# Forgetting attention moved whole beside the projections, and RWKV's units started every ten rounds

## The reference

```python
z = h @ w_in                         # columns: fox (1544), rwkv (1792), gates (2048)
# forgetting attention ("fox"): 8 heads of 64, causal
q = rmsnorm(q, g_q); k = rmsnorm(k, g_k)
c = cumsum(log_sigmoid(zf_last + b_f))
pr = softmax(where(mask, q @ k.T * scale + c[q] - c[k], NEG_BIG))
y_fox = pr @ v
# RWKV-7: 8 heads of 64
zr = zr + mu_shift * (token_shift(zr) - zr)
decay, a, kk, k, v, r = ...          # small low-rank products, elementwise
st = st * w_t + (st @ a_t) b_t + v_t k_t ;  y_t = st @ r_t   # recurrence over tokens
y_rwkv = (group_norm(y) + bonus) * g
merged = sigmoid(zg0) * (y_fox @ w_o_fox) + sigmoid(zg1) * (y_rwkv @ w_o_rwkv)
```

## Time and profile before

| | |
|---|---|
| three runs | 4293.16, 4296.64, 4302.06 us; median 4296.64 |
| profiled execution | 4300.37 us, span of the core 4299.1 us |
| mean granted TensorE clock | 0.938 of full |
| PE busy | 3922.4 us, 91% |
| DVE, ACT, POOL busy | 2143.1, 1157.1, 330.0 us |
| `gates` with 96 rounds of fox | 2438 to 2692 us |
| RWKV with 132 rounds of fox | 2702 to 3245 us |

### The profile page before, as it was taken

The page is one execution under the profiler, slowest core; times in us unless marked ns, Lnnn a source line. Parts: engine busy times, 40 slices in busy tenths (PEclk is TensorE's granted clock), DMA queues, the critical chain, the costliest instruction groups (busy, mean ns, idle before and its releaser), DMA issues. The chain is left out here.

```text
span 4299.1 us, 75536 instructions
## 1 busy us (share of the span) xinstructions
PE 3922.4 (91%) x33542; PEld 3206.1 (75%) x33542; DVE 2143.1 (50%) x3525; ACT 1157.1 (27%) x1597; POOL 330.0 (8%) x362
## 2 busy tenths in 40 slices
PE   6999959986998999999999999778887999999999
PEld 5788837774876888888798677566666788888877
DVE  4633345554433444445624333465554476666774
ACT  4221234442322312121400222242323321111122
POOL 0001102230000000000000000232311000000000
PEclk8999969997998999999999899888787999999999
DMA  5212120114112111111132312201004311111111
GB/s 179 87 52 69 50 84 6 32 32 150 49 40 98 48 51 40 50 48 49 51 133 96 125 67 84 87 23 56 22 10 149 108 48 41 49 49 49 50 45 64
DMA packets 213721, 281.99 MB, mean 66 GB/s; under 512 B 15612, under 2 KB 171004, under 8 KB 213268
## 3 DMA queue, kind: packets, MB, share of 16 engines
q1 hardware_dynamic: 177536, 191.35, 13.8%
q10 hardware_dynamic: 35860, 85.79, 5.3%
HBM read 217.11 MB, written 60.00 MB: 64 GB/s over the span
## 5 line engine op out<-in xcount | busy, mean ns | idle before, releaser
L436 PE MATMUL ps<-sb_a_h,sb_whi 128*128 128x512 f32 x2912 | 1164.5, 400 | 51.0 <-DVE sb_a_h L665 44.6
L437 PE MATMUL ps<-sb_a_h,sb_wlo 128*128 128x512 f32 x2912 | 1146.1, 394 | 0.0
L438 PE MATMUL ps<-sb_a_h,sb_whi 128*128 128x512 f32 x2912 | 1145.5, 393 | 0.0
L436 PEld LDWEIGHTS ps<-sb_a_h,sb_whi 128*128 128x128 f32 x2912 | 552.8, 190 | 195.1 <-issue 53.3
L438 PEld LDWEIGHTS ps<-sb_a_h,sb_whi 128*128 128x128 f32 x2912 | 553.2, 190 | 118.6
L437 PEld LDWEIGHTS ps<-sb_a_h,sb_wlo 128*128 128x128 f32 x2912 | 553.5, 190 | 116.9 <-issue 4.3
L389 ACT ACTIVATE sb_whi<-sb_wraw 128x2048 fp32r<-128x2048 f32 (+3 forms) x146 | 260.4, 1783 | 839.7 <-PE ps L438 512.8
L397 DVE TENSOR_TENSOR sb_wlo<-sb_wraw,sb_whi 128x2048 fp32r<-128x2048 f32 (+3 forms) x146 | 315.8, 2163 | 241.5 <-ACT sb_whi L389 216.0
L548 DVE TENSOR_TENSOR sb_x<-sb_x,ps 128x512 f32<-128x512 f32 x480 | 313.3, 683 | 227.0 <-PE ps L438 224.5
L436 PE MATMUL ps<-sb_a_g,sb_whi 128*128 128x512 f32 x896 | 349.8, 390 | 10.5 <-DVE sb_x L548 10.5
L437 PE MATMUL ps<-sb_a_g,sb_wlo 128*128 128x512 f32 x896 | 348.8, 389 | 0.0
(11 more groups left out here) (513 smaller groups left out, 5567.2 us busy)
## 6 DMA issues: line engine op xcount, KB each, us to landing
sb_wraw<-w_in SPq DMA_DIRECT2D x33, 1024.0 KB, 5.1
sb_wraw<-w_ff SPq DMA_DIRECT2D x32, 1024.0 KB, 5.3
sb_wraw<-w_up SPq DMA_DIRECT2D x22, 1024.0 KB, 5.0
sb_wraw<-w_down SPq DMA_DIRECT2D x11, 1024.0 KB, 4.8
sb_wraw<-w_xkv SPq DMA_DIRECT2D x8, 1024.0 KB, 5.5
sb_wraw<-w_out SPq DMA_DIRECT2D x8, 1024.0 KB, 5.3
sb_a_f<-y ACTq DMA_DIRECT2D x16, 512.0 KB, 4.6
gates<-sb_a_f ACTq DMA_DIRECT2D x32, 256.0 KB, 2.0
```

The source lines that it names most:

```text
L436: e.matmul(o, wh[:, k, c], xh[:, sl], start=(k == 0), stop=False)
L437: e.matmul(o, wl[:, k, c], xh[:, sl], start=False, stop=False)
L438: m = e.matmul(o, wh[:, k, c], xl[:, sl], start=False, stop=(k == t.nk - 1))
```

## The change

Fox is advanced beside the later `shift` tiles (`later = shift[3:]`, 25 tiles) and all 32 `gates` tiles, four rounds per tile (after k = 1, 3, 5 and 7), and what is left of it is run out before RWKV begins. The staging buffers of the projections go from 8 to 6, the banks of `shift` and `lora` are 0 to 3. In fox, AV has v stationary (64 columns) and the transposed probabilities moving (128 columns), the two heads writing the two halves of the partitions; the result comes out already turned, so the transposes of line 2718 and the division at 2755 go. The division is made in the turn: T is an ordinary product of the probabilities with a diagonal matrix that holds the inverse sums (`DG`), which DVE builds after each exponential. A pair has 55 rounds.

RWKV has no fox beside it. `loop` runs 110 rounds; unit i's `pre` and unit i-1's `inner` start every ten rounds, so for five of ten rounds two `inner` streams run; `scan` starts 25 rounds after its unit's `pre`. M, Y, XA, XT and G1 get a second buffer, the rotated r, O and the bonus a third, the two-bank ring becomes (0, 2), the one-bank ring 4 to 7, and the four empty rounds before `pre` go.

```diff
+            later = shift[3:]
+
+            def four(stream):
+                for _ in range(4):
+                    next(stream, None)
...
                 for t in shift:
-                    pe_fm(e, t, hp)
+                    pe_fm(e, t, hp, None, (0, 1, 2, 3), pe_fox, (1, 3, 5, 7) if t in later else ())
...
                 for t in gates:
-                    pe_fm(e, t, hp, None, (0, 1, 2, 3), pe_fox, (2, 5, 7))
+                    pe_fm(e, t, hp, None, (0, 1, 2, 3), pe_fox, (1, 3, 5, 7))
...
                     if t.first:
                         ve_cut(e, t.j + 2)
+                    if t in later:
+                        four(ve_fox)
                     e.wait_ge(*bk.filled(t.key))
...
                         for b in range(0, n, 128):
-                            m = e.transpose(ps[:, b:b + 128], lg_of(p, qb, g)[:, a + b:a + b + 128], C("ident"))
+                            m = e.matmul(ps[:, b:b + 128], lg_of(p, qb, g)[:, a + b:a + b + 128], DG[g], start=True, stop=True)
...
-                    for j in range(qb + 1):
-                        m = e.matmul(bk["fx_y", p, qb // 4][:, c:c + 64], lg_of(p, qb, g)[:, j * 128:(j + 1) * 128],
-                                     R(VF + j * 128 + g * 64, 64), start=(j == 0), stop=(j == qb))
+                for j in range(qb + 1):
+                    for g in range(2):
+                        m = e.matmul(bk[key][64 * g:64 * g + 64, c:c + 128], R(VF + j * 128 + g * 64, 64),
+                                     lg_of(p, qb, g)[:, j * 128:(j + 1) * 128], start=(j == 0), stop=(j == qb))
...
+                for g in range(2):
+                    e.wait_ge(*fx_exp[g].at(8 * p + qb))
+                    e.reciprocal(sinv[:, g:g + 1], R(SUM + (qb % 4) * 2 + g, 1)).then_inc(*vo.up())
+                    e.wait_ge(*vo.last())
...
+                    e.tensor_scalar(DG[g], C("ident"), sinv[:, g:g + 1], None, ALU.mult).then_inc(*fx_dg[g].up())
...
             a4(*fox)
+            for stream in fox:
+                for _ in stream:
+                    pass
             meet()
...
-            RW_REST = 4
+            RW_REST = 0
...
-                for i in range(10):
-                    streams = [scan(i - 2)] if i >= 2 else []
-                    if 1 <= i <= 8:
-                        streams.append(inner(i - 1))
-                    if i < 8:
-                        streams.append(pre(i))
-                    together(*streams, side=fox)
+                running = []
+                for n in range(110):
+                    i, begins = divmod(n, 10)
+                    if n % 10 == 5 and n >= 25 and i - 2 < 8:
+                        running.append((0, scan(i - 2)))
+                    if begins == 0 and 1 <= i <= 8:
+                        running.append((i, inner(i - 1)))
+                    if begins == 0 and i < 8:
+                        running.append((99, pre(i)))
+                    running.sort(key=lambda x: x[0])
+                    for x in list(running):
+                        if next(x[1], running) is running:
+                            running.remove(x)
```

More of the change, by code:

```diff
@@ L2420, in ve_a4 @@
                         ve_cut(e, t.j + 2)
-                    three(ve_fox)
+                    four(ve_fox)
                     e.wait_ge(*bk.filled(t.key))
@@ L2452, in ac_a4 @@
                                     b[0:rows, :]).then_inc(*o.up())
+                for t in first[-2:]:
+                    e.wait_ge(*stored(t.key))
+                e.wait_ge(*x_spilled.at(0))
                 for t in shift:
@@ L2493, in po_a4 @@
                 e.memset(AF[:, 4 * T:4 * T + 3078], 0.0).then_inc(*sh_pad.up())
-                for t in gates:
-                    three(po_fox)
+                for t in later + gates:
+                    four(po_fox)
             def sp_a4(e):
@@ L2499, in sp_a4 @@
                 e.dma_start(WU[64:128, :], D["w_aaa_up_2"]).then_inc(*lora_in.up())
-                sp_load(e, shift[-1].j + 3)
+                sp_load(e, shift[0].j + 3)
                 e.wait_ge(*x_spilled.at(0))
-                e.wait_ge(*bk.filled(shift[-1].key))
-                for t in first[-8:]:
+                for t in first[-6:]:
                     e.wait_ge(*stored(t.key))
-                for t in gates:
+                for t in later + gates:
                     if t.first:
                         sp_load(e, t.j + 3)
-                    three(sp_fox)
+                    four(sp_fox)
             pe_a4(pe), ve_a4(ve), ac_a4(ac), po_a4(po), sp_a4(sp)
@@ L2643, in ve_block @@
                 yield
+                for g in range(2):
+                    e.wait_ge(*fx_exp[g].at(8 * p + qb))
+                    e.reciprocal(sinv[:, g:g + 1], R(SUM + (qb % 4) * 2 + g, 1)).then_inc(*vo.up())
+                    e.wait_ge(*vo.last())
+                    if p or qb:
+                        last = (p, qb - 1) if qb else (p - 1, 7)
+                        e.wait_ge(*bk.filled(("fx_t", *last, g, chunks(last[1])[-1][0])))
+                    e.tensor_scalar(DG[g], C("ident"), sinv[:, g:g + 1], None, ALU.mult).then_inc(*fx_dg[g].up())
                 for a, n in chunks(qb):
@@ L3423, in b2, with loop @@
-            loop(lambda i: pe_pre(pe, i), lambda i: pe_in(pe, i), lambda i: pe_scan(pe, i), fox[0])
-            loop(lambda i: ve_pre(ve, i), lambda i: ve_in(ve, i), lambda i: ve_scan(ve, i), fox[1])
-            loop(lambda i: ac_pre(ac, i), lambda i: ac_in(ac, i), lambda i: ac_scan(ac, i), fox[2])
-            loop(lambda i: po_pre(po, i), lambda i: po_in(po, i), lambda i: po_scan(po, i), fox[3])
+            def loop(pre, inner, scan):
+                running = []
[11 more added lines that the diff above has]
+                            running.remove(x)
+                assert not running
```

183 lines of the change are left out of this document (83 added, 100 removed).

## The result

The kernel after takes 4349.64 us (median of 4 runs, 4344.79 to 4351.09) against 4298.80 us for the kernel before, run beside it (4293.16 to 4302.06): a ratio of 1.0118, 95% interval 1.0100 to 1.0135. I had forecast 4286, slightly faster. It is slower, outside the forecast's own 4255 to 4320 and just at the upper end of the wide range, 4350. The profiled execution took 4348.74 us against 4300.37, 48 us more, and all of it lies in the two stages that the change touches.

The account below looks back on a forecast made before the run. PE alone was taken to bound the projections, a PE, DVE, PE chain RWKV's `inner`. Projections +190 (streams +102, pauses +88) and RWKV -200 gave -10 on a profiled 4300.4: 4286 us predicted, own range 4255 to 4320, 8 in 10 4215 to 4350.

Parts of the forecast that it names:

- Part 1, streams (+102): Projection stage: fox's PE instructions take 39 us a pair, 156 for four pairs, against 54 in the stage before: +102.
- Part 1, pauses (+88): Projection stage: switches, block waits, heads, casts and half-clock time, less overlap, against 26 us before: +88.
- half-clock time, 8: Projection stage, a term of the pauses: some time at half clock after the long stops, 8 us.
- blocks, heads and casts: Projection stage: block waits 16, pair heads 38, casts 14 beside `gates`, 29 beside `shift`, other `shift` pairs 7, less 15 overlap.
- Part 2, the period (38 us): RWKV: six periods of 38 us with two `inner` streams, bounds 33 and 45, making 228 us instead of 385.4.
- The head: RWKV's first twenty rounds: 29 us for `pre` alone, then 26 us for `pre` and one `inner`.
- the tail: RWKV's end, the last `inner` and two `scan`: 60 us, against 57.6 before.
- B: Projections: casts beside `shift` close DVE and ACT to fox, PE's clock falls, stage grows by 250: +50, 4347; chance 0.17.
- C: RWKV: the period stays at 45 us, DVE's and PE's work in one in-order chain: total +32, 4329; chance 0.12.
- A: RWKV: two units abreast interlock fully, 33 us a period, heads and casts cost half: -80, 4217; chance 0.21.
- D: Fox is not done beside the projections; the rest runs alone before RWKV and the -10 gain is gone; chance 0.02.
- Drain ahead of AV 0.35: Projection stage, a sign: PE idles 0.35 us ahead of AV's 16 instructions as the array's shape changes.

Follow-up runs that it names:

- e2: Kernel after, with T as transposes against the identity; diagonal still built and waited for, division left out of the result: 4324.05 us, ratio 1.0037.
- e4: Kernel after, whole computation, with T as transposes and the division made late, as DVE multiplies the turned output by the inverse sums: 4293.53 us, ratio 0.9978.
- e8: e4 with one DVE instruction of RWKV's preparation, the key times the inverse norm, issued one round later: 4295.16 us, ratio 0.9981.
- e10: e5 with two overwritten 128x128 products put ahead of PE's wait for DVE in each of a unit's five levels: 4266.21 us, ratio 0.9909.
- e12: e5 with `pre` ahead of the two `inner` streams in each RWKV round instead of behind them: 4273.96 us, ratio 0.9930.
- e5: e4 with the weight casts' subtraction on POOL instead of DVE as long as fox runs: 4263.75 us, ratio 0.9909.
- e6: e4 with two of the turned tiles copied out three times by DVE in RWKV, 22 us of added work: 4298.53 us, ratio 0.9994.

## Why the prediction was wrong

**Direction and size.** The sum was right in most of its parts and wrong in one quantity that I had at nearly nothing: PE's clock. From the profiled 4300.4 the forecast was 4290, measured 4348.7: 58 us. By the windows +30 is in the projections (220 against 190), +39 in RWKV (161 against 200), and -10 the stretch that the window of before leaves out. With the projections counted to the meeting of the engines in both, they are +21 and +39.

**Part 1, streams (+102): borne out.** At full clock T's four blocks take 0.9 us from start to start (two rows of the timeline of PE, one head each):

```profile
2891.71 1.05 PE L2603 MATMUL ps<-sb_b,sb_x 128*128 128x128 f32 x8
2892.60 1.06 PE L2603 MATMUL ps<-sb_b 128*128 128x128 f32 x8
```

AV is 0.055 us an instruction at full clock where I took 0.045 with the tails, 0.067 over the stage. Fox's streams, from start to start without waits, sum to 166 us (T 76, S 43, AV 39, sums of squares 9) against 54 in the stage before, to the meeting: +112. The excess is the clock: at 0.225 us a block T would be 65. e2 takes 36 us off T's stream, where I had T cost 8.2 x 4 = 33 more, and the stage gives back 21 of them: PE idles 5 us more in e2, and the projections' own matmuls take 10 us longer.

**Part 1, pauses (+88): the waits right, the term "half-clock time, 8" wrong.** PE's idle time sums to 79 us against 17, +62. I had 16 + 38 + 14 + 29 + 7 - 15 = 89 for blocks, heads and casts; the casts' share, read from the ten stops that end at a cast, is 42, against 14 + 29. The projections' own 1368 matmuls take 357 us, 48 more than at 0.226 each, where I had 17 for switches and 8 for the clock; before, to the meeting, they took 321. At full clock they start 0.244 us apart on average against 0.231 before, which is 18 of those 35 us. At the lower level they start some 0.45 apart, and that is the other 17. It isn't all that the clock cost, since fox's own instructions lie at the lower level too. Of PE's busy time 93 us lie there, before 25. Half of such time is lost, 34 us more than before, where the forecast had 8. So the clock was 26 us over, more than the whole miss of 21; without it my sum for this stage was 5 us too high. That is the failed step: I counted each stop once, as idle time, and next to nothing for the slow stretch behind it.

**Part 2, the period (38 us): wrong, by the clock and the idle both.** I wrote that PE's work would be "about 31 at the clock of 0.91", a clock read from the one stretch before without `pre` or fox, and added 7. Measured are 33.8 of work at 0.83, and 9.3 idle. Of the 33.8, 13 stand at the lower level, so at full clock it would be 27.3: the work was right, the clock was not. In the profiled executions of e4 to e8, e10 and e12 the idle time of a period stays between 7.7 and 9.5 us, whatever was added or moved; extra PE work counts 75%, extra DVE work about a third, fewer rounds nothing. What holds that idle time there isn't shown. The head was 8 us over (63 against 55), the tail about right (61 against 60); the five periods and what lies of a sixth ahead of the tail carry 30 of the 39 us.

**Rivals.** B (casts close DVE and ACT to fox, 4347) has the number, by luck: it adds a stage 250 us longer (measured 211 to 220) to an RWKV 200 shorter (161). Its mechanism is there, 42 us of stops and 30 us for taking the subtraction away (e5), but the stops were in my sum already at 43, they last 1.7 to 5.8 us and not 6 to 8, and its point of decision, pauses over 140 us, was not reached (79 idle). What B said in passing, that the clock falls, is what was missing. C (period 45, +32) is nearest for RWKV, 43, and not for its reason: with DVE's and PE's work in one chain e6 would have cost its full 22 us, not 7 (15 at most). A is out: no stretch came near 33. D is out.

**What would show it.** PE busy never under 85% in the projections: held for the whole, 87%, but not for its parts, 82% over each of the first two 100 us. Waits over 100 us: 79, missed. Largest on the diagonal and the sums of squares: held. Drain ahead of AV 0.35: the 0.35 us are there, but they are not PE's (the rows below). Period 38: missed, and just at the bound of 43 that I gave for being wrong. The drain, in the kernel after (start us, us, instruction, idle ahead):

```profile
2861.42 0.40 PE L438 MATMUL ps<-sb_a_h,sb_whi 128*128 128x512 f32 x1
2861.75 0.13 PEld L2616 LDWEIGHTS ps<-sb_x 128*64 128x64 f32 x1 [0.36 <-issue]
2861.75 0.32 PE L2616 MATMUL ps<-sb_x 128*64 128x128 f32 x1
```

The 0.36 us with nothing to wait for stand on the weight loads (PEld). The last projection matmul is still at work then, and PE's own row has no idle time; the 0.36 us of line 2586 in the earlier trace rows stand on a weight load too, and I had read them as PE's. From the start of the last projection matmul to the first of AV it is 0.33 us instead of 0.226, and from the last of AV to the next projection matmul 0.20 instead of 0.055: about 0.25 us a visit. AV comes to 9.7 us a pair all the same, against my 9.3, since its instructions take 0.055 us and not 0.045. The Trainium skill, "TensorEngine Tiling (Array Packing)", "Key Properties", has a change of tiling mode drain the array; the weight loads' wait on nothing agrees. Under "Performance Considerations" it lists this swap with 2x column tiling; AV's instruction went from 0.107 to 0.055 us at full clock, which agrees too, with 8 visits a pair at 0.25 us to set against it.

**What stays open.** In the projections the time at the lower clock goes with PE's idle time. In RWKV the sum of the idle time doesn't tell the clock: over five periods it is 40 us at 0.80 (e8), 43 at 0.81 (e12), 42 at 0.84 (e5), 48 at 0.89 (e6, one execution, with the highest clock of its twelve) and 39 at 0.89 (e10). e10 shows that filling pauses raises the clock. Whether it is where the pauses fall or what PE does when busy that sets it otherwise wasn't told apart.

## What to carry to other kernels

Where PE is the bound and its work is fed by short chains, price each added stop of PE twice: its length, and the work behind it at half clock; in this stage some 34 us came behind 62 us of added stops. Before moving a side stream beside other work, list what stands at the head of each in-order queue that it shares, with the wait that it brings: here a 2.2 us cast that waited 2.5 us for ACT held up a 0.3 us instruction that PE needed, and moving it to an idle engine twice as slow won 30 us. Move fold-ins (here a division) only where their operands are ready early; in the chain between exponential and turn, with the second pass that it brought, it cost 50 us of the stage, behind the product 7.

## What the runs showed of the hardware

The scatter between executions of one kernel goes with TensorE's mean clock. Of 29 executions of the kernel before on one chip the two with the lowest mean clock, 0.933, took 4314.8 and 4315.4 us and the fastest, 4293.2 us, had 0.939; over them the correlation is -0.84, and a thousandth of the mean clock is worth 2.3 us. A single execution of the kernel before was off its median by up to 8 us below and 15 above on this chip, and by 22 below on another. e6's profiled one, 4287.75 us at a clock of 0.945, taken alone would have made extra DVE work a gain of 6 us over e4's median.

POOL's long subtractions did DVE no harm that shows. With the casts' subtractions moved (31.0 us of DVE's work in e4), DVE's busy time in the projections went from 209.2 us in e4 to 179.0 in e5, 30.2 less, so its other work took no more than 1 us longer beside 62 us of POOL's.
